# First chunks behind five norms multiply weighted, not normed, tiles, and the root is applied to their result

## The reference, cut to what matters

```python
def _rms_norm(x, g):
    y = xf * lax.rsqrt(jnp.mean(xf * xf, axis=-1, keepdims=True) + EPS)
    return (y * g.astype(jnp.float32)).astype(x.dtype)
def _modulate(xn, shift, scale):
    return xn * (1 + scale[:, None, :]) + shift[:, None, :]
def _swiglu(x, w_in, w_out):
    gate, up = jnp.split(x @ w_in, 2, axis=-1)
    return (jax.nn.silu(gate) * up) @ w_out
def first_block(...):
    cond = jax.nn.silu(c)
    for l in range(DEPTH):
        mod = cond @ ada_w[l] + ada_b[l]
        sh1, sc1, g1, sh2, sc2, g2, sh3, sc3, g3 = jnp.split(mod, N_MOD, axis=-1)
        hn = _modulate(_rms_norm(h, norm_g[l, 0]), sh1, sc1)
        h = h + 0.5 * g1[:, None, :] * _swiglu(hn, ffn1_w_in[l], ffn1_w_out[l])
        hn = _modulate(_rms_norm(h, norm_g[l, 1]), sh2, sc2)
        z = hn @ w_in[l]
        ...   # from z: differential attention, convolution, spatial gating, forgetting attention
        h = h + g2[:, None, :] * (mixed @ w_out[l])
        hn = _modulate(_rms_norm(h, norm_g[l, 2]), sh3, sc3)
        h = h + 0.5 * g3[:, None, :] * _swiglu(hn, ffn2_w_in[l], ffn2_w_out[l])
```

## Time and profile before

| | |
|---|---|
| runs | 1911.7, 1917.17 and 1919.98 us, median 1917.17 |
| the profiled execution | 1920.41 us, its span in the trace 1918.6 us |
| mean granted TensorE clock | 0.991 of full speed |
| TensorE busy | 1857.8 us, 97% of the span |
| GpSimd busy | 1437.8 us, 75% |
| ScalarE busy | 988.4 us, 52% |
| VectorE busy | 913.4 us, 48% |

### The profile page before, as it was taken

One profiled execution on the slowest core, in us unless ns is written; L12 is line 12 of the kernel. 1 busy time (PEld: TensorE's weight loads), 2 busy tenths in 40 slices (PEclk: granted clock), 3 DMA queues, 4 the chain that ended last, 5 costly groups with the idle time before them and its releaser, 6 DMA issues.

```text
span 1918.6 us, 37038 instructions
## 1 busy us (share of the span) xinstructions
PE 1857.8 (97%) x15544; PEld 1804.0 (94%) x15544; DVE 913.4 (48%) x1817; ACT 988.4 (52%) x1531; POOL 1437.8 (75%) x660
## 2 busy tenths in 40 slices
PE   6999998999999999889999999999999999999999
PEld 3999997999999998879999998999999999999999
DVE  3675597475148478854121634343311634343321
ACT  2544466544454445664445445575554444575543
POOL 1888872788878887548888965588898964588896
PEclk9999999999999999999999999999999999999999
DMA  9999752695689886436645643365664643455662
GB/s 315 360 348 302 258 182 82 224 366 182 193 301 367 301 296 187 132 132 221 195 156 183 215 153 116 131 194 176 198 198 159 216 154 111 132 189 179 193 210 88
DMA packets 357077, 397.94 MB, mean 207 GB/s; under 512 B 9016, under 2 KB 319024, under 8 KB 356912
## 3 DMA queue, kind: packets, MB, share of 16 engines
q1 hardware_dynamic: 356752, 395.38, 62.8%
q10 hardware_dynamic: 160, 0.20, 0.1%
HBM read 394.51 MB, written 1.05 MB: 206 GB/s over the span
## 4 chain that ended last, share of the span: by engine, by line
PE 86%; DVE 4%; SPq 3%; ACT 3%; DMA 2%; POOL 2%; issue 1%; ACTq 0%; DVEq 0%
PE bank L729 77%; POOL w_lo L695 2%; PE bank L1006 1%; PE bank L964 1%; SPq L590 1%; PE bank L760 1%; PE bank L764 1%; PE bank L761 1%; SPq L557 1%; ACT arena L1396 1%; SPq L554 1%; SPq L600 1%; PE bank L720 1%; DMA arena<-in_ada_w 1%; DMA ring<-in_ffn_w_in 1%
## 5 line engine op out<-in xcount | busy, mean ns | idle before, releaser
L695 POOL TENSOR_TENSOR w_lo<-ring,w_hi 128x1024 fp32r<-128x1024 f32 (+2 forms) x656 | 1437.6, 2218 | 465.9 <-ACT w_hi L1258 465.5
L1258 ACT ACTIVATE w_hi<-ring 128x1024 fp32r<-128x1024 f32 (+2 forms) x656 | 628.9, 983 | 401.7 <-PE bank L729 377.6
L729 PE MATMUL bank<-hn,w_hi 128*128 128x256 f32 x2752 | 772.0, 281 | 9.4 <-ACT arena L1575 4.9
L729 PE MATMUL bank<-hn,w_lo 128*128 128x256 f32 x2752 | 764.8, 278 | 0.0
L729 PE MATMUL bank<-hn_lo,w_hi 128*128 128x256 f32 x2752 | 764.7, 278 | 0.0
L729 PEld LDWEIGHTS bank<-hn,w_hi 128*128 128x128 f32 x2752 | 518.7, 188 | 14.7 <-ACT arena L1575 6.5
L729 PEld LDWEIGHTS bank<-hn,w_lo 128*128 128x128 f32 x2752 | 519.3, 189 | 0.0
L729 PEld LDWEIGHTS bank<-hn_lo,w_hi 128*128 128x128 f32 x2752 | 517.5, 188 | 0.9 <-issue 0.5
L729 PE MATMUL bank<-gated,w_hi 128*128 128x256 f32 x1408 | 244.4, 279 | 1.2 <-POOL w_lo L695 1.2
L729 PEld LDWEIGHTS bank<-gated,w_hi 128*128 128x128 f32 x1408 | 213.7, 188 | 1.4 <-POOL w_lo L695 1.4
L729 PE MATMUL bank<-gated,w_lo 128*128 128x256 f32 x704 | 196.1, 279 | 0.0
(11 more groups left out here) (237 smaller groups left out, 2433.4 us busy)
## 6 DMA issues: line engine op xcount, KB each, us to landing
ring<-in_ffn_w_in SPq DMA_DIRECT2D x88, 1024.0 KB, 7.4
ring<-in_w_in SPq DMA_DIRECT2D x72, 1024.0 KB, 5.2
arena<-in_ada_w SPq DMA_DIRECT2D x35, 2048.0 KB, 10.9
ring<-in_w_up SPq DMA_DIRECT2D x32, 1024.0 KB, 5.5
ring<-in_w_down SPq DMA_DIRECT2D x32, 1024.0 KB, 5.2
ring<-in_ffn_w_out SPq DMA_DIRECT2D x32, 768.0 KB, 5.4
ring<-in_ffn_w_out SPq DMA_DIRECT2D x32, 640.0 KB, 4.1
ring<-in_w_in SPq DMA_DIRECT2D x16, 512.0 KB, 3.7
```

Source lines behind the costliest of these rows:

```text
L695: pool.tensor_tensor(w_lo[:, q, ks], ring[:, r, k0:k0 + n], w_hi[:, q, ks], ALU.subtract) \
L729: last = mm(out, a, b, start=start and i == 0, stop=stop and i == 2)
L1258: f(w_hi[:, q, half * 4:half * 4 + n], ring[:, r, k0:k0 + n], ACT.Copy).then_inc(weights_rounded, 1)
```

## The change

It concerns the norms of z and f2 in both layers and of f1 in layer 1 (f1 of layer 0 stays as it was).

1. h times the gain (`der`) alone is made ahead, two k-tiles behind each group of the out product or of the output projection (`weigh_ahead` on ScalarE, `weighed` on VectorE). The shift is written as two more columns of the tile, its rounded part and the rest (`shift_columns`; `hn_wide` has S + 16 columns).
2. The first chunk multiplies these tiles with 258 columns (`weighted_product`), into banks 0 and 7. The norm's sum stands behind the products of k 0 and 1.
3. The normed tiles are made as before, into the same `hn`, while the first chunk runs. The second chunk takes them k by k. `settle` is one transpose ahead of the third chunk.
4. `apply_root` on VectorE adds up the two shift columns of the result and multiplies the rest by the root of each token. For FFN in, Silu then takes the shift's sum as its bias; for z, the convolution's input adds it.
5. `Z_UNITS`: ca and cg are now one chunk each, and dv and fq come in two half chunks (before: ca and cg in two halves each). `gated_scale(8, ...)` moves from behind f1 into its head.
6. In block two the columns of roots by token come from two transposes of 128 columns instead of two products of one column.

```diff
-Z_UNITS = (("ca", (0, 1), 768, False), ("cg", (2, 3), 1024, False), ...
-           ("dv", (6,), 512, True), ("fq", (7,), 1792, False), ...
+Z_UNITS = (("ca", (0,), 768, False), ("cg", (1,), 1024, False), ...
+           ("dv", (4, 5), 512, True), ("fq", (6, 7), 1792, False), ...
-        hn, hn_lo = sb("hn", KT, S, dtype=F32R), sb("hn_lo", KT, S, dtype=F32R)
+        hn_wide, hn_lo = sb("hn", KT, S + 16, dtype=F32R), sb("hn_lo", KT, S, dtype=F32R)
+        hn = hn_wide[:, :, 0:S]
TensorE
+            def settle(dst):
+                pe.transpose(dst, ident, ident)
+            def weighted_product(phase, n, outs):
+                pe.wait_ge(vector_done, eng.at(f"h {n} {4 if n == 'f2' else 6}"))
+                for half in range(2):
+                    half_ready(phase, 0, half)
+                    for k in range(4):
+                        kx = 4 * half + k
+                        if kx == 2:
+                            norm_sum(n)
+                        pe.wait_ge(scalar_done, eng.at(f"weighted hi {n} {kx}"))
+                        for c in range(2):
+                            ws = slice(c * P, (c + 1) * P)
+                            mm(outs[c], w_hi[:, 0, kx, ws], hn_wide[:, kx, 0:S + 2], ...)
+                            mm(outs[c], w_lo[:, 0, kx, ws], hn_wide[:, kx, 0:S + 2], ...)
+                        pe.wait_ge(vector_done, eng.at(f"weighted split {n} {kx}"))
+                        for c in range(2):
+                            last = mm(outs[c][:, 0:S], w_hi[:, 0, kx, c * P:(c + 1) * P], hn_lo[:, kx], ...)
...
-                    last = mm(bank[:, 7, t:t + 1], rstd[0:1, t * P:(t + 1) * P], ones[0:1, 0:1], ...)
+                    last = pe.transpose(bank[:, 7, t * P:(t + 1) * P], rstd[:, t * P:(t + 1) * P], ident)
...
-                norm_sum("z")
...
-                            first="z" if i == 0 else None,
+                            first="z" if i == 1 else None, settled=i == 2,
ScalarE
+            def weighted_and_norm(n, phase, shift):
+                take_squares(n, (6, 7))
+                weigh_ahead(n, (6, 7))
+                norm_root(n)
+                f(rstd[:], rstd[:], ACT.Exp, scale=-0.5).then_inc(scalar_done, eng.step(f"token rstd {n}"))
+                for k in range(KT):
+                    act.wait_ge(vector_done, eng.at(f"normed k {n} {k}"))
+                    if k in (0, 4):
+                        act.wait_ge(weights_used, eng.at(f"used {phase} 0" if k else f"half used {phase} 0"))
+                    f(hn[:, k, :], normed[:, k % 2], ACT.Identity, bias=mod[:, shift + k:shift + k + 1]) ...
+                    if k == 1:
+                        round_half(phase, 1, 1)
+                    if k == 4:
+                        act.wait_ge(weights_in[slot_of(phase, 2)], eng.arrived(phase, 2))
+                        round_half(phase, 2, 0)
+                    if k == 6:
+                        round_half(phase, 2, 1)
...
+                    if p == 0 and not whole:
+                        round_chunk(s + "in", 3)
+                        act.wait_ge(vector_done, eng.at(f"root applied {s}"))
+                        for c in range(2):
+                            f(act_tmp[:, 0, c * S:(c + 1) * S], bank[:, 0, c * S:(c + 1) * S], ACT.Silu,
+                              bias=small[:, 60 + c:61 + c]) ...
...
VectorE
+            def shift_columns(at_):
+                shifts = mod[:, at_:at_ + 8]
+                dve.tensor_copy(hn_wide[:, :, S], shifts) ...
+                tt(hn_wide[:, :, S + 1], shifts, hn_wide[:, :, S], ALU.subtract) ...
+            def apply_root(n, phase, c1):
+                dve.wait_ge(weights_used, eng.at(f"used {phase} 0"))
+                dve.wait_ge(scalar_done, eng.at(f"token rstd {n}"))
+                for c, b in enumerate((0, 7)):
+                    dve.tensor_reduce(small[:, 60 + c:61 + c], bank[:, b, S:S + 2], AX.X, ALU.add) ...
+                for dst, b in ((bank[:, 0, 0:S], 0), (c1, 7)):
+                    tt(dst, bank[:, b, 0:S], rstd[:], ALU.mult) ...
...
+                if following != "z2 0":
+                    shift_columns({"z": 24, "f1": 0}[following])
+                if following == "z":
+                    gated_scale(8, 32, R_NORM_G + 8, layer) ...
...
                 scale_norm("z", lambda k: col(der, 8 + k), 24)
+                apply_root("z", "z", bank[:, 7, 0:S])
                 ada_fold(layer, 1)
                 modulation(layer, 48, 64)
                 gated_scale(16, 56, R_NORM_G + 16, layer).then_inc(vector_done, eng.step())
+                shift_columns(48)
...
-                tt(yp[:, :, CONV_K - 1:CONV_K - 1 + S], bank[:, 0].rearrange(...), cg[:], ALU.mult) ...
+                for c, b in enumerate((0, 7)):
+                    stt(yp[:, c, CONV_K - 1:CONV_K - 1 + S], bank[:, b, 0:S], small[:, 60 + c:61 + c], cg[:, c, :],
+                        ALU.add, ALU.mult) ...
```

More of the change, by code:

```diff
@@ L754, in product @@
                         half_ready(phase, i, half)
+                        if settled and half == 0:
+                            settle(outs[0][:, 0:P])
                         for k in range(n if first else 0):
@@ L1301, in weigh @@
                     if k >= 2:
-                        act.wait_ge(vector_done, eng.at(f"split {n} {k - 2}"))
-                    gain = norm2[:, gain_at + k:gain_at + k + 1]
+                        act.wait_ge(vector_done, eng.at(f"{tag}split {n} {k - 2}"))
+                    gain = gains[:, k:k + 1]
                     f(normed[:, k % 2], h[:, k], ACT.Identity, scale=gain).then_inc(scalar_done, eng.step())
-                    f(hn[:, k, :], h[:, k], ACT.Identity, scale=gain).then_inc(scalar_done, eng.step(f"hi {n} {k}"))
@@ L1307, in norm, with weigh_ahead @@
-            def norm(n, phase, shift=None, begun=False, late=()):
-                if not begun:
-                    norm_root(n)
+                    f(hn[:, k, :], h[:, k], ACT.Identity, scale=gain).then_inc(scalar_done, eng.step(f"{tag}hi {n} {k}"))
+            def weigh_ahead(n, ks):
+                if n in ("z2 0", "z2 1"):
+                    layer = int(n[-1])
+                    weigh(n, ks, norm2[:, 8 * layer:8 * layer + 8])
+                elif n != "final":
+                    at_ = {"f1": 0, "z": 8, "f2": 16}[n]
+                    weigh(n, ks, der[:, at_:at_ + 8], "weighted ")
@@ L1312, in norm @@
+            def norm(n, phase, shift, late=()):
                 for k in range(KT):
                     act.wait_ge(vector_done, eng.at(f"normed k {n} {k}"))
[L1315 to L1320, removed]
+                    f(hn[:, k, :], normed[:, k % 2], ACT.Identity, bias=mod[:, shift + k:shift + k + 1]) \
+                        .then_inc(scalar_done, eng.step(f"hi {n} {k}"))
+                    for at_k, i, half in late:
@@ L1331, in squares_and_norm, with ffn @@
                 round_half(phase, 1, 0)
[L1332 to L1339, removed]
+            def ffn(s, following, whole=False):
                 functions("silu_and_others")
```

123 lines of the change are left out of this document (77 added, 46 removed).

## The result

| | before | after |
|---|---|---|
| median of 5 runs each | 1914.18 us (1911.7 to 1919.98) | 1944.17 us (1943.78 to 1945.79) |
| ratio to before | | 1.0138, 95% interval 1.011 to 1.0165 |
| span of the profiled execution | 1918.6 us | 1942.1 us |

The forecast was 1921 us, at most 1931. The time is outside the range, above all that was priced. First the waits of PE in the changed kernel (what waited, for whom: us in total, times, longest).

What follows compares the result with a forecast made beforehand. TensorE was taken as the bound nearly everywhere, with losses at the norms. Terms f1 and f2 -11.6, out product +0.6, z +14.2, block two +0.5 summed to +3.7, giving 1921 us; 8-in-10 range 1907 to 1931.

Steps and rivals of the forecast that it cites:

- The norms: Five changed norms, sum's start to 97th product: 12.9 us each in f1 and f2 (saving 11.6), 12.8 in z (10.5).
- half clock: TensorE at 1.2 GHz instead of 2.4 for 3.41 us behind a wait; expected gone at norms, present behind conv mean.
- z up to the mean: In each z stage VectorE delays the conv mean: it starts at about 305.5 instead of 300.11, 5.4 us later.
- Conv input: VectorE's input to z's convolution: expected at 260.6 (258.7 to 265.4), neither gain nor loss though dq starts 5.3 earlier.
- POOL's splits: GpSimd's splits late in z come 5.0 us earlier, 291.3 to 296.1 and 296.8 to 301.5, meeting VectorE's forget operations.
- The forget operations: VectorE's seven forget gate operations, held by GpSimd's splits ahead of the mean, end 3.2 to 6.3 us late; 5.5 taken.
- Behind the mean: The product after TensorE's wait at the conv mean runs at half clock, losing 1.7 us per layer (0.8 to 3.2).
- 258 columns instead of 256 in 160 products are priced by columns: 0.15 us in all.: First chunks' products with two shift columns cost only by column count, 0.15 us in all.
- The single pace of 0.113: TensorE products throughout the program priced at 0.113 us each, from a run of 1536 taking 174.08 us.
- 0.25 more in each layer: Block two: two transposes of 128 columns replacing two one-column products cost 0.25 us per layer, 0.5 in all.
- Layer 1's first out product: Three more small VectorE operations at this stage's head, where weights already land late, cost 0.6 us.
- z and gv: Each z stage, half clock behind the mean included, ends 7.1 us later than before: +14.2 in both layers.

Runs made afterwards that it cites:

- before_wide: The kernel before with only hn's tiles set 272 words apart instead of 256; 1937.29 us, ratio 1.0093.
- after_narrow: The changed kernel with normed tiles 256 words apart over the same memory and f2's shift columns written in the output projection; 1915.14 us, ratio 0.9985.

## Why the prediction was wrong

**The norms: right.** Predicted 12.9 us for f1 and f2, measured 12.75; 12.8 for z, measured 13.6, the rest in short waits of the second chunk for its tiles. No half clock fell on any of the five.

**z up to the mean: right, step by step.** Conv input predicted at 260.6, made from 260.00 to 260.81. POOL's splits predicted from 291.3 and 296.8, seen at 291.06 and 296.71. The forget operations end at 302.32, 6.1 later than before, where I said 5.5. The mean predicted at 305.5 came at 305.90. The Trainium skill (SBUF — State Buffer, "Who interferes with whom") has an operation with two SBUF inputs blocked by a running GpSimd operation that reads SBUF, and the scan has two such inputs; by that I had 6.3. The trace agrees: the scan took 2.75 us instead of 0.69.

**Behind the mean: too small.** Predicted a loss of 1.7 in gv from the half clock; measured 1.9. Not predicted was a second fall in attention, 2.3 us in either layer. Windows of the changed kernel; the clock is the last column but two:

```profile
299.58:309.82 10.24, 3.92 (x14) 3.57 (x15) 7.14 (x15) 0.63 (x1) 1.94 (x1) 0.50 0.40 135
330.30:337.13 6.83, 5.93 (x22) 3.73 (x21) 4.37 (x18) 4.07 (x15) 0.00 (x0) 0.50 0.00 0
```

Such a fall comes without any wait at the mean as well: before_wide took 27.44 us for layer 1's attention. And the wait comes without the fall: in after_narrow's layer 1 PE waited 11 us at the mean and attention took 25.2, as before. So the fall is not charged to the wait alone, and what decides it stays open.

**The step that failed: "258 columns instead of 256 in 160 products are priced by columns: 0.15 us in all."** The tile's two more columns were priced only where they are read. Their true price is the pitch they force on all of hn, some 8900 products with `hn` or `hn_lo`: 29 us here, by after_narrow, and 18 in the kernel before, by before_wide. The 29 are more than what was lost against the kernel before, since that ran partly at the slow pace too, and the narrow tile behind the transposes is fast there as well (block two 863.45 against 868.8). The single pace of 0.113 that I took from the earlier trace rows for the whole program was the second half of the error: the trace of before had both, and I didn't look at f2 of layer 1, where the same chunks took 113.07.

**Smaller terms.** Of the root columns I wrote "0.25 more in each layer"; with the narrow tile the sign is wrong: they gained 5.3 us (1920.49 against 1915.14), and 144 products of z2 behind them ran at 0.1133 instead of 0.1178. Layer 1's first out product was not 0.6 slower: it took 59.9 us in the changed kernel and 61.15 with the narrow tile, against 61.29 before. Together: norms -21.1, z and gv +26.7 (predicted +24.8), attention +4.5, and +13.4 in all other stages, for which the prediction had 1.1.

## What to carry to other kernels

When a tile in on-chip memory gets wider, count every instruction that reads it, not only those that read the new part: its pitch moves all rows, and here that cost more than the wait that the change removed. Keep such columns in the shared memory under a second view, so that the frequent reader keeps its pitch. And compare the pace of one product between stages of the same trace before pricing any: two values at one clock mean that something unpriced sets it.

## What the runs showed of the hardware

Back-to-back products of 256 float32r columns with a weight load each run at 0.1133, 0.1178, 0.1188 or 0.1200 us at full clock, by the byte place of `hn` (and the tiles behind it), while the weights' tiles stay where they are. At the place 192 two paces are possible (0.1133 and 0.1178), at 128 and 384 two others (0.1188 and 0.1200); one product more can change one into the other, and a pace keeps for over a thousand products. With the roles swapped, so that the weights' tile is the moving one, the same place of `hn` gives nearly the same paces (0.1133, 0.1178, 0.1186, 0.1200). So the moving tile's own place doesn't set them. Whether it is the distance of the two tiles, or the place of `hn` in either role, is open, since the weights never moved. Equal paces at 0 and 256 and at 128 and 384 speak for a period of 256 bytes, which no run tests by itself.

The Trainium skill (SBUF — State Buffer, "Who interferes with whom") lists TensorE's read ports for moving operand and weights as independent, and says that TensorE never waits on anyone. By that I would expect no effect of the place; the measurement, 1892 against 1966 us, decides otherwise, though it doesn't say what conflicts.

VectorE's operations from SBUF to SBUF are held up by GpSimd's splits, the scan among them: the seven of the forget gate span 2.9 us alone and 9.8 beside the splits (the scan 0.69 and 2.75).
